# First attention: the next query product one head earlier, in a PSUM bank of its own, and GpSimd's work in shorter instructions

## The reference, cut to what matters

```python
q = rmsnorm_2(q.reshape(B, S, A_HEADS, A_HEAD_DIM), q_gain)
k = rmsnorm_2(k.reshape(B, S, A_KV_HEADS, A_HEAD_DIM), k_gain)
scores = jnp.einsum('bnqkgd,bnskd->bnkgqs', q, kb) * scale + bias   # 4 blocks of 128 rows
m = jnp.maximum(jnp.max(scores, axis=-1, keepdims=True), sink)
p = jnp.exp(scores - m)
denom = jnp.sum(p, axis=-1, keepdims=True) + jnp.exp(sink - m)
o = jnp.einsum('bnkgqs,bnskd->bnqkgd', p / denom, vb).reshape(B, S, 1024)
return o @ w_out
```

## Time and profile before

| | |
|---|---|
| profiled execution | 2904.75 us, its span 2903.5 us |
| PE busy | 2771.9 us (95%), 13671 matmuls |
| DVE busy | 1542.9 us (53%) |
| ACT busy | 975.6 us (34%) |
| POOL busy | 247.8 us (9%) |
| mean granted TensorE clock | 0.966 of full |
| first attention | about 1273 to 1467 us of the span |

### The profile page before, as it was taken

How to read it: one execution, slowest core, us unless ns; L and a number is a source line. 1 busy time by engine, 2 the same in 40 slices (tenths; PEclk the granted TensorE clock), 3 DMA queues, 4 the chain that set the end, 5 groups by cost and what they waited for, 6 DMA issues and landing times.

```text
span 2903.5 us, 33346 instructions
## 1 busy us (share of the span) xinstructions
PE 2771.9 (95%) x13671; PEld 2327.1 (80%) x13671; DVE 1542.9 (53%) x2569; ACT 975.6 (34%) x1621; POOL 247.8 (9%) x285
## 2 busy tenths in 40 slices
PE   7899999999999999998999999999998888899999
PEld 5788788888777888888878888888887777788887
DVE  4635446574656455466664444543445576653433
ACT  3334234342443222235542222322224444432321
POOL 2000010000020000023310000100002222300000
PEclk9999999999999999998999999999998788999999
DMA  4322234523223637672223322333221000033231
GB/s 133 102 87 79 82 102 131 184 87 102 85 75 100 86 101 106 88 104 89 79 93 102 98 91 87 102 102 102 96 79 51 15 24 30 29 116 102 88 98 62
DMA packets 280175, 259.06 MB, mean 89 GB/s; under 512 B 40516, under 2 KB 276055, under 8 KB 280023
## 3 DMA queue, kind: packets, MB, share of 16 engines
q1 hardware_dynamic: 280023, 256.93, 30.7%
HBM read 242.23 MB, written 14.68 MB: 88 GB/s over the span
## 4 chain that ended last, share of the span: by engine, by line
PE 83%; DVE 11%; ACT 4%; issue 1%; POOL 1%; SPq 0%; DMA 0%; DVEq 0%; POOLq 0%; ACTq 0%
PE bank L1033 27%; PE bank L1034 26%; PE bank L1035 26%; DVE Wl L1672 1%; PE bank L1176 1%; PE bank L1044 1%; ACT Wh L1342 1%; DVE Pl L2123 1%; DVE X L1878 1%; ACT Z L1602 1%; DVE sm L2115 1%; DVE TMP L1865 1%; DVE TMP L1862 1%; DVE Pl L1660 1%; DVE nt L1645 1%
## 5 line engine op out<-in xcount | busy, mean ns | idle before, releaser
L1033 PE MATMUL bank<-Hh,Wl 128*128 128x512 f32 x2144 | 851.8, 397 | 17.4 <-DVE Hl L1688 17.4
L1034 PE MATMUL bank<-Hl,Wh 128*128 128x512 f32 x2144 | 842.9, 393 | 0.0
L1035 PE MATMUL bank<-Hh,Wh 128*128 128x512 f32 x2144 | 841.9, 393 | 0.0
L1342 ACT ACTIVATE Wh<-RAW 128x1024 fp32r<-128x1024 f32 (+2 forms) x454 | 441.0, 1022 | 434.6 <-PE bank L1035 391.1
L1672 DVE TENSOR_TENSOR Wl<-RAW,Wh 128x1024 fp32r<-128x1024 f32 (+1 forms) x420 | 494.5, 1221 | 169.5 <-ACT Wh L1342 169.0
L1033 PEld LDWEIGHTS bank<-Hh,Wl 128*128 128x128 f32 x2144 | 408.4, 190 | 106.1 <-issue 10.3
L1035 PEld LDWEIGHTS bank<-Hh,Wh 128*128 128x128 f32 x2144 | 407.7, 190 | 86.3
L1034 PEld LDWEIGHTS bank<-Hl,Wh 128*128 128x128 f32 x2144 | 408.3, 190 | 84.5 <-issue 1.7
L1033 PE MATMUL bank<-Ph,Wl 128*128 128x512 f32 x1168 | 461.8, 395 | 12.8 <-DVE Pl L1754 3.5
L1034 PE MATMUL bank<-Pl,Wh 128*128 128x512 f32 x1168 | 457.6, 392 | 0.0
L1035 PE MATMUL bank<-Ph,Wh 128*128 128x512 f32 x1168 | 457.4, 392 | 0.0
(11 more groups left out here) (260 smaller groups left out, 2754.5 us busy)
## 6 DMA issues: line engine op xcount, KB each, us to landing
RAW<-in_ffn_wg SPq DMA_DIRECT2D x44, 1024.0 KB, 5.1
RAW<-in_ffn_wu SPq DMA_DIRECT2D x44, 1024.0 KB, 5.2
RAW<-in_ffn_wd SPq DMA_DIRECT2D x32, 1024.0 KB, 5.1
RAW<-in_w_up SPq DMA_DIRECT2D x22, 1024.0 KB, 5.1
RAW<-in_w_in SPq DMA_DIRECT2D x20, 1024.0 KB, 5.1
RAW<-in_ffn_wd SPq DMA_DIRECT2D x16, 768.0 KB, 4.3
bias_scratch<-M SPq DMA_DIRECT2D x16, 512.0 KB, 8.0
RAW<-in_w_down SPq DMA_DIRECT2D x8, 1024.0 KB, 5.4
```

The lines of the kernel that those rows point to most:

```text
L1033: mm(o, ll, rh, start=start, stop=False)
L1034: mm(o, lh, rl, start=False, stop=False)
L1035: return mm(o, lh, rh, start=False, stop=stop)
L1342: run(Wh[:, n % 3, x:y], RAW[:, n % 2, x:y], ACT.Copy).then_inc(*w_hi.up(("w_hi", n, i)))
```

## The change

The products of the loop come one turn earlier (`q_product(6+i)`, with number 5 before the loop) and have one bank of their own, `products`. The query turns stand first in their turns of the loop, `q_out(5+i)` stands second, and `a_q_norm` is a step of its own behind `a_norm` in turns 2, 6 and 10. The ring for query turns and output units has two banks. The first product of a group now falls in turns 2 and 6 (it fell in 3 and 7), and the `split` that it calls falls there with it. On GpSimd each half of a weight's low part is done in two instructions, in both attentions, and a head's division in four (one for each block) in place of two.

```diff
-        banks.take(("aq", g, b))
+        (products[0] if products else banks).take(("aq", g, b))
 ...
-        if b == 3:
-            do("a_q_norm", g)
 ...
     for u in range(4):
         q_product(u)
         q_out(u)
+    do("a_q_norm", 0)
     q_product(4)
     for g in range(2):
         banks.take(("a_kt", g))
         do("a_k_turn", g)
+    products.append(banks.part(1))
+    q_product(5)
     q_turn(0)
     q_out(4)
     scored, turned, summed = banks.part(2), banks.part(2), banks.part(1)
 ...
     for i in range(16 + LV):
+        if i % 4 == 3 and i < 15:
+            q_turn(i // 4 + 1)
+        if i < 11:
+            q_out(5 + i)
         if i < 16:
 ...
         if 0 <= i - LT < 16:
             turns(i - LT)
-        if i % 4 == 3 and i < 15:
-            q_turn(i // 4 + 1)
-        if i < 11:
-            q_product(5 + i)
+        if i < 10:
+            q_product(6 + i)
         if i >= LV:
             values(i - LV)
         if i < 16:
             do("a_exp", i)
             do("a_norm", i)
+        if i % 4 == 2 and i < 11:
+            do("a_q_norm", i // 4 + 1)
         if i >= LV and (i - LV) % 2:
             attended((i - LV) // 2)
-        if i < 11:
-            q_out(5 + i)
         if i >= LO:
             out_units(2)
 ...
-    for ring in (scored, turned, summed):
+    for ring in (scored, turned, summed, products[0]):
         banks.join(ring)
 ...
-                        tt(Wl[:, n % 3, x:y], RAW[:, n % 2, x:y], f(Wh[:, n % 3, x:y]), ALU.subtract).then_inc(
-                            *w_lo_pool.up(*([("w_lo", n)] if i else [])))
+                        m = (x + y) // 2
+                        for x, y in ((x, m), (m, y)):
+                            ins = tt(Wl[:, n % 3, x:y], RAW[:, n % 2, x:y], f(Wh[:, n % 3, x:y]), ALU.subtract)
+                        ins.then_inc(*w_lo_pool.up(*([("w_lo", n)] if i else [])))
 ...
-                tt(S[:, 0:128], S[:, 0:128], rs[:, 0:1].broadcast_to([128, 128]), ALU.mult)
-                v = S[:, 128:896].rearrange("p (n s) -> p n s", n=3)
-                tt(v, v, rs[:, 1:4].unsqueeze(2).broadcast_to([128, 3, 256]), ALU.mult).then_inc(
-                    *pool_out.up(("a_scaled", h)))
+                for n, (z0, z1) in enumerate(SEG):
+                    ins = tt(S[:, z0:z1], S[:, z0:z1], rs[:, n:n + 1].broadcast_to([128, z1 - z0]), ALU.mult)
+                ins.then_inc(*pool_out.up(("a_scaled", h)))
```

More of the change, by code:

```diff
@@ L646, in attend_a_order @@
     do("a_bias", 1)
-    tile = {}
+    tile, products = {}, []
     def q_product(u):
```

## The result

The changed kernel takes 2925.66 us (median of six runs, 2920.91 to 2927.64), against 2908.39 for the kernel before in six (2903.17 to 2915.51): 1.0053 times as long, 95% interval 1.0034 to 1.0073. It is slower: the loss is small, but the whole interval lies above 1, and the fastest run of the changed kernel is slower than the slowest of the one before. The kernel before spreads over 12 us, and the three runs that the prediction started from had their median 5 us under that of the six.

The account below looks back on a forecast made before the run. TensorE, holding 83% of the chain of waits, was taken to bound the kernel through its waits and clock. Terms -7.8 + 7.4 + 4.3 + 8.4 = +12.3 us on 2904.75, less 1.4 for the median, gave 2915 us, range 2901 to 2924.

Parts of the forecast that it names:

- Start: Around query turn 0: idle time 3.8 us in place of 6.9, low clock of 4.7 us gone; 7.8 us gained.
- the signs that were to show the forecast right: Profile after: idle about 2, 9, 7.6, 5.6 us, last released by addition to X; clock above 0.5 from 1310 to 1318.
- Query turns 1 and 2: Waits for the query norm of 9.05 and 7.6 us in place of 3.31 and 3.00; costs 7.4 and 4.3 us.
- the rival in which it stays hidden: Turns 2 and 6: ScalarE splits in idle time, pieces miss the norm; +5.8 us, 2909 us; chance 0.15.
- Query turn 3: Wait of 5.6 us in place of 0.19, released by the addition to X; with low clock costs 8.4 us.
- the price of the low clock: Time lost to low clock behind query-turn waits: 3.2, 3.0, 3.0 us at turns 1 to 3, none at the start.
- The rival "longer low clock": Three long waits cost 4.7 us of low clock each, perhaps also the start: about 2923 us; chance 0.27.
- GpSimd's pieces: Shorter GpSimd instructions in both attentions: about 0.2 us earlier at the start, nothing in the second attention within 1 us.
- the rule weighed in the prediction: One-input reciprocal of a_norm might pass busy GpSimd: norm of turns 2 and 6 1.2 us earlier each, sum +9.9 us.
- The rival "faster": Norm starts by 3 us into turns 2, 6, 10; waits under 1 us, about -19 us, 2884 us; chance 0.08.

Follow-up runs that it names:

- experiment 5: Changed kernel with the weight splits and loads of turns 2 and 6 moved behind the product of turns 3 and 7: 2924.80 us, one run.
- experiment 4: Changed kernel with the query turns back behind scores and turns, as before the change: 2917.97 us, ratio 1.0031 to the kernel before.
- experiment 3: Changed kernel with the query norm directly behind a_soft, ahead of a_norm, in turns 2, 6 and 10: 2916.18 us, ratio 1.0025 to the kernel before.
- experiment 6: Changed kernel with the products' bank given back to the ring of query turns and output units at turn 11: 2923.54 us, one run.
- experiment 2: Kernel before with only GpSimd's shorter instructions: 2910.22 us, ratio 1.0011 to the kernel before.
- experiment 7: Changed kernel with norm ahead of a_norm, splits in turns 0 and 4, products' bank given back at turn 11, short GpSimd instructions: 2902.62 us, ratio 0.9983.
- experiment 8: The kernel of experiment 7 with GpSimd's long instructions of before: 2901.20 us, ratio 0.9974 to the kernel before.
- experiment 1: Changed kernel (new order and banks) with GpSimd's instructions of before: 2927.45 us, ratio 1.0057 to the kernel before.
- experiment 9: The kernel of experiment 8 with the query turns back behind scores and turns: 2891.10 us, ratio 0.9936 to the kernel before.

## Why the prediction was right or wrong

The direction, the mechanism and its places were right. The time was under by 10.7 us (2915 for 2925.66), and the range's upper end by 1.7. Of the 10.7, 5.0 are the kernel before, whose median of six is that much above the median of three that the forecast started from. Taken against the kernel before in the same runs, 12.3 us were forecast and 17.3 measured (9.9 to 21 by the ratio's interval); in the first attention, which is where the forecast put all of it, 14.8.

- *Start.* Waits of 2.1 and 1.4 us were forecast, 2.27 and 1.13 came. The gain of 7.8 us rested on a clock that stays high; it fell at about 1309 and cost 2.8 us. So of the 4.7 us of low clock only 1.9 went, and the start was worth 5.4 us by the same sum. Of the signs that were to show the forecast right, this is the one that failed: the granted clock was 0.50 from 1310 to 1314.
- *Query turns 1 and 2.* Forecast 9.05 and 7.6 us, came 8.67 and 7.33. They grew by 5.4 and 4.3 us over 3.31 and 3.00. The moved `split` makes 3.4 us of each (experiment 5), so the rival in which it stays hidden is out, and the earlier asking 2.5 (experiment 4). Together that is 0.5 and 1.6 us more than the growth; what in the change gave that back wasn't taken apart. The early norm is the other way to take it out, but alone it gives 3.3 and 3.5, since it meets the `split` (experiment 3).
- *Query turn 3.* Forecast 5.6 us and a release by the addition to X; came 5.25, so released. The two banks are 1.3 us of it (experiment 6), the earlier asking 2.5 (experiment 4); the other 1.3 of the 5.1 us of growth wasn't taken apart.
- *The term that was mis-sized* is the price of the low clock: 1.7, 0.1 and 3.0 us more than before were put at the three turns, which was 3.2, 3.0 and 3.0 in all; it was 3.5, 4.4 and 3.8, and 2.8 at the start in place of none. In sum the low clock cost 14.5 us after, where I had 9.2, and about 9 before. The rival "longer low clock" had the right mechanism and is where the time came out (about 20 us more than before by its sum). Idle time grew from 14.3 to 24.6 us, by 10.3; the forecast's 13.8 before leaves out the wait of 0.54 us in the row below. With 5.5 us more of low clock that makes 15.8, where the attention grew by 14.8; PE's busy time in it grew by 4.5, so the prices step by step are about 1 us too high in sum.
- *GpSimd's pieces.* Forecast as nothing in all and 0.2 us at the start. The runs show no more: the medians with short instructions are 1.9 us above those without in the old order (experiment 2, interval 0 to 6 us) and 1.4 in the order of experiments 7 and 8. The reason given holds: a chain of small instructions passes one for each piece, so four pieces hold up four, and the norm in front of query turn 0 took 7.8 us with four pieces and 7.9 to 8.0 with two. The reciprocal did pass a busy GpSimd, in 0.18 us, where I had put 1.2 us more. That agrees with the rule weighed in the prediction: the Trainium skill, "SBUF — State Buffer", section "SBUF: two separate sides", names VectorE instructions with two SBUF inputs or in a two-port mode as those that the lock holds up, and the reciprocal has one input. But it gained next to nothing: the norm's first instruction, right behind it, took 1.10 us until the same piece ended, and the wait was 0.4 us under the forecast, not 1.2.
- *The rival "faster"* named the point from which it decides, a norm that starts by 3 us into the turn. In experiment 3 the norm did start 2.9 us into turn 2 (1323.08, scores at 1320.19), and that was not enough: it also took the `split` out of the turn, the third bank, and the query turns behind the scores.

The wait that 13.8 leaves out, in PE's timeline of the kernel before:

```profile
1414.44 0.50 PE L1033 MATMUL bank<-Ph,Wl 128*128 128x512 f32 x1 [0.54 <-DVE Pl L1998]
```

Open: the part from the second attention on took 707 to 717 us in the profiles (711.8 in experiment 1, with the instructions of before, against 707.4), and the kernel before varies by 12 us from run to run. In that attention PE was idle 56.7 us of 350.0 before and 52.4 of 354.6 after, at a mean granted clock of 0.83 and 0.81:

```profile
2200.00:2550.00 350.00, 293.30 (x1799) 258.58 (x1798) 226.08 (x582) 150.17 (x384) 86.79 (x89) 0.83 0.09 29
```

```profile
2216.40:2571.00 354.60, 302.24 (x1797) 268.53 (x1796) 224.95 (x581) 150.15 (x384) 89.34 (x107) 0.81 0.09 28
```

So it is clock rather than waiting; what sets it off in one run and not in another wasn't tried. Nor was a kernel in which only the products come earlier, so the start's share of the gain in experiments 7 to 9 is read from the waits and not from a run of its own.

## What to carry to other kernels

To start a product earlier buys nothing if its result is also asked for earlier: look at where the chain between them (here a norm of twelve small instructions and a product) stands in its engine's queue, and keep independent work in front of the instruction that asks. A step that calls others moves them with it; here a weight's split landed on the exponentials and the norm that the next query turn waits for. Price a wait of TensorE at its length and the low clock behind it: here 3.5 to 4.4 us on top of waits of 5 to 9 us, and 2.8 behind two waits of 2.3 and 1.1 us close together.

## What the runs showed of the hardware

Waits of 2.27 and 1.13 us with transposes between them brought the 1.2 GHz level until about 1315, and 2.14 us of idle time in experiment 7 did so too; 0.93 and 0.56 us in experiment 9 did not. Around 2 us the length alone didn't decide: the same wait of 1.82 us between the halves of query turn 3 was followed by a granted clock of 0.67 and then 0.50 in experiment 8 (1400 to 1404 us), and by full clock in experiment 7. Cutting GpSimd's instruction in four holds up a chain of small VectorE instructions as long as one in two does: four times 1.2 us against twice 2.3; the whole chain was 0.1 to 0.2 us shorter. A GpSimd instruction on 512 columns takes 1284 ns, so four of them take 0.2 to 0.3 us more than two of 1024.
